# Moving the second row gathers, the activation loads and one norm step in a two-layer mixer and expert kernel

## The chip, the cores and the metric

The kernel runs on one core of a Trainium2 chip. Its engines are TensorE (PE in the profile; its weight loads PEld), VectorE (DVE), ScalarE (ACT), GpSimd (POOL) and SyncE (SP); each runs its own list of instructions in order and meets the others at semaphores. 16 DMA engines move data between the chip's main memory and the on-chip memory; here SyncE issues nearly all plain loads and stores, ScalarE the stores of the gate matrices, and GpSimd the row gathers. The metric is the device time of one execution in microseconds, the median of several.

## What is computed

Two layers over 512 tokens of width 1024, everything in float32. Each layer takes a modulation (shift, scale, gain) from `silu(c) @ ada_w`, runs a token mixer (a chunked state-space scan, a multi-scale pool and stick-breaking attention), and then a product-key expert layer, which is where most of the time goes:

```python
sc = jnp.einsum('thid,hikd->thik', q, keys)          # 8 heads, two halves of 128 keys
top_s, top_i = lax.top_k(sc, 16)
... # top 16 of the 16 x 16 sums, softmax over them: experts (of 16384) and gates
act = jnp.einsum('thkd,td->thk', u_tab[eb], hb)
coef = gb * jax.nn.gelu(act, approximate=False)
out = jnp.einsum('thk,thkd->td', coef, v_tab[eb])
```

So each token uses 128 (8 x 16) of 16384 experts, each with a row of `u_tab` and one of `v_tab`.

## The kernel before

**Tiling.** All tokens stand as columns, and weights come as a stream of tiles of 128 x 1024 (512 KB), 298 a layer: 18 for the input projection, 8 for the output projection, 16 for the queries, 128 for `u` (the U stage, from `U0`) and 128 for `v` (the V stage, from `EV0`). A tile of float32 is split in two parts of float32r: ScalarE writes the high part (`hi`, line 693), VectorE the low part (`lo`, line 1519), and TensorE multiplies three times (high by high, high by low, low by high), 24 matmuls for a tile of the V stage (`v_block`, line 1478).

**Two ways for the experts.** 144 of the 512 tokens (128 and `EXTRA` = 16) go by gathers: GpSimd fetches for each the rows of `u` and of `v` that it needs (`gather`, line 657), 144 gathers of 128 rows of 4 KB (512 KB) for each table and layer, into a ring of five buffers; VectorE multiplies and sums them (`gather_u` line 1998, `gather_v` line 2010). The other 368 tokens (`TD`) go densely through all 16384 experts: the U stage makes their activations, stores them (`activations` in main memory) and builds dense gate matrices (stored too); the V stage reads both back for a group of four tiles (`GROUP`) at a time, multiplies them to coefficients (`coefs`, lines 2101 to 2105), splits these (`c_hi` line 945, `c_lo` line 2111) and multiplies them with the tiles of `v`.

**The V stage on VectorE.** Iteration b does, in this order: the coefficients of tile b+2, one or two gathers (`V_GATHERS[b]`; 144 over 126 iterations, so 18 iterations have two), the low part of the coefficients of b+2, and the low part of weight tile b+2. Before the change the iterations with two are those with b % 7 == 2, that is 2, 9, 16 and so on to 121.

**The order on SyncE.** `load_w(l, n)` has three buffers (`RAWS`): it waits until both parts of tile n-3 are made, so tile b of the V stage is issued at the end of VectorE's iteration b-5. `load_acts(l, g)` (736 KB, line 548) has two buffers and waits until the coefficients of the group two back are made (`s_cp`); `load_gates` (512 KB, line 554) stands right behind it and has no wait of its own there. In the V stage both stand ahead of `load_w` for the tiles 6, 10, 14 and so on. Writing a tile's number as 4m+1, 4m+2 and so on, the group m+1 is loaded, before the change, between the loads of tiles 4m+1 and 4m+2:

```python
if EV0 + 6 <= n < STREAM - 2 and (n - EV0 + 2) % GROUP == 0:
    load_acts(l, (n - EV0 + 2) // GROUP)
    load_gates(l, (n - EV0 + 2) // GROUP)
load_w(l, n)
```

The wait of `load_acts` for group m+1 is for the coefficients of tile 4m-1, which VectorE makes at the start of iteration 4m-3.

**The start.** In layer 0 the first third of the modulation is a product with eight chunks of `adaw` (1 MB each, `ada_chunk`, line 1035, in the order `FIRST_ADA` = 0, 2, 1, 4, 3, 6, 5, 7). `norm_groups` (line 1000) sums the squares of x, ScalarE and VectorE make the inverse root, and `norm_rows` (line 1007) spreads it over the partitions. After the last chunk ScalarE copies the sums (`ada_rows`, line 726), TensorE transposes them (`modulation`, line 1046), and VectorE makes the scales (line 1579) and the normed and modulated columns (lines 1537 and 1545), for which it needs both `modulation` and `norm_rows`; `project_pair` (line 986) multiplies them with the first two weight tiles. VectorE stands at the low part of weight tile 1 before it waits for `modulation`.

Of the kernel before, what the change touches and what calls it, by code (L numbers as in the profile page):

```python
# [34 lines left out]
N_KEYS = 128  # L35
# [3 lines left out]
EV0 = U0 + N_KEYS  # L39
STREAM = EV0 + N_KEYS  # L40
# [14 lines left out]
FIRST_ADA = (0, 2, 1, 4, 3, 6, 5, 7)  # L55
# [13 lines left out]
GROUP = 4  # L69
# [52 lines left out]
    U_GATHERS[_n] = 2 if _n % 3 == 2 else 1  # L122
U_GATHERS[GATHER0] += UG - sum(U_GATHERS)
assert sum(U_GATHERS) == UG and U_GATHERS[N_KEYS - 1] == 0, sum(U_GATHERS)
V_GATHERS = [0] + [2 if _b % 7 == 2 else 1 for _b in range(1, N_KEYS - 1)] + [0]
assert sum(V_GATHERS) == UG


# [55 lines left out]
def build(nc, xT, cT, final_g, adaw, wst, params, keysT, u_0, u_1, v_0, v_1, g_dram, a_dram, outT):  # L184
    u_rows, v_rows = (u_0, u_1), (v_0, v_1)
    ctx = ExitStack()
    with ctx:
# [332 lines left out]
        @block.sync  # L520
        def _(sp):
            sp.dma_start(cond[:, :], cT).then_inc(s_cin, 16)
            for h in range(2):
                half = slice(h * KT // 2, (h + 1) * KT // 2)
                sp.dma_start(x[:, half, :], xT[:, half, :]).then_inc(s_in[h], 16)

            def load_w(l, n):

                g = l * STREAM + n
                if g >= RAWS:  # L530
                    sp.wait_ge(s_wh, g - RAWS + 1)
                    sp.wait_ge(s_wl, g - RAWS + 1)
                sp.dma_start(w_raw[:, g % RAWS, :], wst[l, n]).then_inc(s_raw[g % RAWS], 16)

            def store_act(l, p):

                sp.wait_ge(s_taken, l * TAKEN + p * 2 + (U0 + 4))
                sp.dma_start(a_dram[p], act_out[:, p % 2, :, :]).then_inc(s_ast[p % 2], 16)

            def load_acts(l, g):  # L540

                s = g % 2
                if g >= 2:

                    sp.wait_ge(s_cp, l * N_KEYS + (g - 1) * GROUP)
                for q in range(2):
                    sp.wait_ge(s_ast[q], (l * GROUPS + g + 1) * 16)
                sp.dma_start(act_in[s][:, :, :, :], a_dram[g * 2:g * 2 + 2].rearrange("q p b t -> p q b t")
                             ).then_inc(s_ain[s], 16)

            def load_gates(l, g):

                s = g % 2
                sp.dma_start(gates[s][:, :, :, :],
                             g_dram[:, :, g * GROUP:(g + 1) * GROUP, :].rearrange("c p b t -> p c b t")
                             ).then_inc(s_gin[s], 16)

            sp.dma_start(par[:, :], params[0]).then_inc(s_par, 16)
            for k in (1, 3, 5):
                sp.dma_start(ada_place(k), adaw[0, k]).then_inc(s_ada0[k], 16)  # L560
            load_w(0, 0)
            sp.dma_start(ada_place(7), adaw[0, 7]).then_inc(s_ada0[7], 16)
            load_w(0, 1)
            load_w(0, 2)
            sp.dma_start(fin_g[:, :], final_g).then_inc(s_fgin, 16)

            for l in range(LAYERS):
                for n in range(0 if l > 0 else RAWS, STREAM):
                    if l > 0 and n == RAWS:

                        sp.wait_ge(s_gate, l + 1)
                        sp.dma_start(par[:, :], params[l]).then_inc(s_par, 16)
                    if n == OUT0 + 5:

                        sp.wait_ge(s_ymix, l + 1)
                        sp.dma_start(keys[:, :, :], keysT[l]).then_inc(s_keys, 16)
                    if n == U0 + GATE1 + 8:

                        for s in range(2):
                            sp.wait_ge(s_gst[s], (l + 1) * (GSTORED // 2) * STORES * 16)  # L580
                        sp.wait_ge(s_gv, (l + 1) * QUADS + 2)
                        load_acts(l, 0)
                    if n == U0 + GATE1 + 10:
                        load_gates(l, 0)
                    if n == U0 + GATE1 + 12:
                        load_acts(l, 1)
                    if n == U0 + GATE1 + 14:
                        load_gates(l, 1)
                    if EV0 + 6 <= n < STREAM - 2 and (n - EV0 + 2) % GROUP == 0:
                        load_acts(l, (n - EV0 + 2) // GROUP)  # L590
                        load_gates(l, (n - EV0 + 2) // GROUP)
                    load_w(l, n)
                    if U0 + 6 <= n < EV0 + 6 and n % 2 == 0:
                        store_act(l, (n - U0 - 6) // 2)
            for k in range(KT):
                sp.wait_ge(s_fin, k + 1)
                sp.dma_start(outT[:, k, :], x[:, k, :]).then_inc(s_ret, 16)
            sp.wait_ge(s_ret, KT * 16)
# [357 lines left out]
        def _(pe):  # L956
# [54 lines left out]
            def norm_rows(m):  # L1011

                pe.wait_ge(s_nroot, m + 1)
                root_rows(bank[2], 0).then_inc(s_rows, 1)
# [7 lines left out]
            for l in range(LAYERS):  # L1022
# [31 lines left out]
                if l == 0:  # L1054
                    ada_chunk(0, FIRST_ADA[3])
                if l == 0:
                    for c in FIRST_ADA[4:]:
                        ada_chunk(0, c)
                norm_rows(2 * l)
                if l == 0:  # L1060
                    modulation(0, 0, 4)

                project_pair(l, 0, l * RHS_PARTS)
# [1182 lines left out]
```

## Time and profile before

| | |
|---|---|
| median of 3 runs | 3026.87 us (3025.02 to 3027.24) |
| the profiled execution | 3027.69 us, its span 3025.8 us |
| TensorE busy | 2944.9 us, 97% of the span |
| VectorE, ScalarE, GpSimd busy | 83%, 48%, 32% |
| V stage of layer 0, of layer 1 | from 1019 to 1537 us, from 2491 to 3012 us |
| moved by DMA | 836.79 MB, 277 GB/s over the span |

A row of a timeline gives the start, the duration, the engine, the line, the operation with what it writes and reads, and in brackets the idle time of the engine before it and what ended that. A busy share is that of the engine's records; records of matmuls in a row overlap, since they are pipelined.

### The profile page before, as it was taken

What the parts mean: (1) busy time and instruction counts of PE and PEld (TensorE: products, weight loads), DVE (VectorE), ACT (ScalarE), POOL (GpSimd) and SP (SyncE); (2) the same over time, 40 slices, a digit from 0 to 9 for tenths busy, and PEclk for the clock granted to TensorE, in tenths of its full rate; (3) what the DMA queues carried; (4) which work ended last, traced back from release to release, by engine and by line L of the source; (5) the groups of instructions that cost most, each with busy time, mean ns of one, the idle gap of its engine ahead of it and who ended that gap; (6) DMA issues with size and microseconds to landing.
All of it is one profiled execution on the core that took longest, in us unless ns stands there. A gap on an engine that the chain in (4) does not pass through costs nothing.

```text
span 3025.8 us, 48999 instructions
## 1 busy us (share of the span) xinstructions
PE 2944.9 (97%) x17798; PEld 2760.8 (91%) x17798; DVE 2524.1 (83%) x4842; ACT 1466.4 (48%) x2347; POOL 956.8 (32%) x709
## 2 busy tenths in 40 slices
PE   6999999999999999999989899999999999999998
PEld 4766789999999999999977678999999999999998
DVE  4666789999897789889876669998989868889888
ACT  3353134488884333333343532446888733333333
POOL 0000026544444333233300000565445433333331
PEclk9999999999999999999999999999999999999999
DMA  7424646799999999999931122569999999999996
GB/s 273 176 91 169 255 143 206 249 331 385 350 358 350 352 360 351 365 357 355 359 102 63 56 70 84 165 204 327 353 386 362 311 379 346 358 360 354 355 359 233
DMA packets 252363, 836.79 MB, mean 277 GB/s; under 512 B 24640, under 2 KB 57664, under 8 KB 241472
## 3 DMA queue, kind: packets, MB, share of 16 engines
q1 hardware_dynamic: 158336, 453.50, 42.3%
q0 software_dynamic: 89280, 348.17, 31.1%
q10 hardware_dynamic: 4608, 33.56, 2.6%
q8 instruction: 52, 0.85, 0.1%
q14 instruction: 87, 0.71, 0.1%
HBM read 751.24 MB, written 83.89 MB: 276 GB/s over the span
## 4 chain that ended last, share of the span: by engine, by line
PE 84%; DMA 6%; DVE 6%; ACT 2%; issue 1%; POOL 0%; SPq 0%; DVEq 0%; ACTq 0%; POOLq 0%
PE banks L970 41%; PE banks L1478 28%; PE banks L1446 4%; DMA w_raw<-wst 4%; PE banks L1284 2%; DVE w_lo L1519 2%; PE banks L986 2%; ACT w_hi L693 1%; PE banks L1035 1%; DMA ring<-u,gidx 1%; PE banks L1369 1%; DMA pj<-adaw 1%; PE banks L1255 1%; DVE vacc L2010 1%; PE banks L1460 0%
## 5 line engine op out<-in xcount | busy, mean ns | idle before, releaser
L693 ACT ACTIVATE w_hi<-w_raw 128x1024 fp32r<-128x1024 f32 x596 | 631.6, 1060 | 842.7 <-PE banks L970 638.2
L1519 DVE TENSOR_TENSOR w_lo<-w_raw,w_hi 128x1024 fp32r<-128x1024 f32 x522 | 639.4, 1225 | 360.8 <-ACT w_hi L693 352.0
L970 PE MATMUL banks<-hH,w_hi 128*128 128x368 f32 (+1 forms) x2528 | 881.5, 349 | 7.7 <-ACT w_hi L693 5.1
L970 PE MATMUL banks<-hH,w_lo 128*128 128x368 f32 (+1 forms) x2528 | 861.1, 341 | 0.0
L970 PE MATMUL banks<-hL,w_hi 128*128 128x368 f32 (+1 forms) x2528 | 860.6, 340 | 0.0
L1478 PE MATMUL banks<-c_hi,w_hi 128*128 128x368 f32 x2048 | 676.4, 330 | 5.7 <-DVE w_lo L1519 5.6
L1478 PE MATMUL banks<-c_lo,w_hi 128*128 128x368 f32 x2048 | 674.3, 329 | 0.0
L1478 PE MATMUL banks<-c_hi,w_lo 128*128 128x368 f32 x2048 | 673.2, 329 | 0.0
L657 POOL DMA_INDIRECT ring<-u,gidx x288 | 419.2, 1455 | 453.6 <-DVE gact L1998 419.0
L657 POOL DMA_INDIRECT ring<-v,gidx x288 | 333.7, 1159 | 694.4 <-DVE vacc L2010 631.7
L970 PEld LDWEIGHTS banks<-hH,w_hi 128*128 128x128 f32 x2528 | 475.4, 188 | 52.8 <-issue 20.7
L970 PEld LDWEIGHTS banks<-hH,w_lo 128*128 128x128 f32 x2528 | 474.9, 188 | 19.6
L970 PEld LDWEIGHTS banks<-hL,w_hi 128*128 128x128 f32 x2528 | 475.7, 188 | 17.4 <-issue 0.5
L1478 PEld LDWEIGHTS banks<-c_hi,w_hi 128*128 128x128 f32 x2048 | 384.4, 188 | 8.8 <-issue 8.8
L1478 PEld LDWEIGHTS banks<-c_hi,w_lo 128*128 128x128 f32 x2048 | 384.5, 188 | 0.0
L1478 PEld LDWEIGHTS banks<-c_lo,w_hi 128*128 128x128 f32 x2048 | 384.4, 188 | 0.0
L945 ACT ACTIVATE c_hi<-htok 128x368 fp32r<-128x368 f32 x252 | 129.6, 514 | 518.7 <-DVE htok L2105 513.3
L2010 DVE SCALAR_TENSOR_TENSOR vacc<-ring,gcoef,vacc 128x1024 f32<-128x1024 f32 x284 | 363.7, 1281 | 3.8
L1998 DVE CUSTOM_DVE_ANT_0 ring<-ring,htok 128x1024 f32<-128x1024 f32 x288 | 344.5, 1221 | 19.8 <-DMA ring<-u,gidx 17.3
L645 POOL TENSOR_TENSOR w_lo<-w_raw,w_hi 128x1024 fp32r<-128x1024 f32 x74 | 177.9, 2405 | 520.5 <-ACT w_hi L693 520.5
L889 ACT ACTIVATE oneh<-oneh,idxT 128x128 f32<-128x128 f32 x736 | 226.2, 397 | 5.8 <-DVE oneh L2020 3.2
L2020 DVE TENSOR_TENSOR oneh<-iota,idxT 128x1024 f32<-128x1024 f32 x184 | 219.7, 1222 | 0.0
(315 smaller groups left out, 2954.0 us busy)
## 6 DMA issues: line engine op xcount, KB each, us to landing
w_raw<-wst SPq DMA_DIRECT2D x596, 512.0 KB
activations<-act_out SPq DMA_DIRECT2D x128, 368.0 KB
act_in<-activations SPq DMA_DIRECT2D x64, 736.0 KB
gate_matrices<-stage ACTq DMA_DIRECT2D x32, 1024.0 KB
gates<-gate_matrices SPq DMA_DIRECT2D x64, 512.0 KB
ada_buf<-adaw POOLq DMA_DIRECT2D x24, 1024.0 KB, 6.9
nrm<-adaw POOLq DMA_DIRECT2D x8, 1024.0 KB, 5.3
pj<-adaw POOLq DMA_DIRECT2D x7, 1024.0 KB, 7.1
```

What stands on the lines that cost most here:

```text
L645: pool.tensor_tensor(w_lo[g % 2][:, :, :].rearrange("p a b -> p (a b)"), w_raw[:, g % RAWS, :], w_hi[g % 2][:, :, :].rearrange("p a b -> p ...
L657: pool.indirect_dma_start(out=ring[:, n % RING, :], out_offset=None, in_=rows[:, :], in_offset=bass.IndirectOffsetOnAxis(ap=gidx[:, k % UG ...
L693: nc.scalar.activation(w_hi[g % 2][:, :, :].rearrange("p a b -> p (a b)"), w_raw[:, g % RAWS, :], ACT.Copy).then_inc(s_wh, 1)
L889: ins = nc.scalar.activation(oh, oh, ACT.Copy, scale=idxT[:, 2, q * QUAD + t:q * QUAD + t + 1])
L945: nc.scalar.activation(c_hi[:, (b + 2) % GROUP, :], coef[:, b % 2, :], ACT.Copy).then_inc(s_chi, 1)
L970: last = mm(bank[s][:, 0:t.stop - t.start], a[s][:, k, :], b[:, k, t], start=(k == 0 and a is w_hi and b is hH), stop=(k == KT - 1 and a i ...
L1446: last = mm(bank[2 + u % 2][:, t * P:(t + 1) * P], oneh[u % OH_SLOTS][:, 0, t, :], oneh[u % OH_SLOTS][:, 1, t, :], start=True, stop=True)
L1478: last = mm(bank[k][:, TG:T], w[j % 2][:, k, :], c[:, j, :], start=(first and w is w_hi and c is c_hi), stop=(final and w is w_lo))
L1519: v.tensor_tensor(w_lo[g % 2][:, :, :].rearrange("p a b -> p (a b)"), w_raw[:, g % RAWS, :], w_hi[g % 2][:, :, :].rearrange("p a b -> p (a ...
L1998: v.tensor_tensor_reduce(ring[:, n % RING, :], ring[:, n % RING, :], rhs[:, :], 1.0, 0.0, ALU.mult, ALU.add, gact[:, k:k + 1]).then_inc(s_ ...
L2010: ins = v.scalar_tensor_tensor(acc[:, :], ring[:, n % RING, :], gcoef[:, k:k + 1], acc[:, :], ALU.mult, ALU.add)
L2020: v.tensor_tensor(oneh[q % OH_SLOTS][:, :, :, :], iota[:, :].unsqueeze(1).unsqueeze(1).broadcast_to(full), idxT[:, 0:2, q * QUAD:(q + 1) * ...
```

## The change

Three edits. The iterations with two gathers of the V stage become those with b % 8 == 1, and 61 and 125 besides (again 18). `load_acts` is issued ahead of the load of tile 4m+1 in place of 4m+2; `load_gates` stays where it was. In layer 0 `norm_rows` stands ahead of the last chunk of the first modulation.

```diff
-V_GATHERS = [0] + [2 if _b % 7 == 2 else 1 for _b in range(1, N_KEYS - 1)] + [0]
+V_GATHERS = [0] + [2 if _b % 8 == 1 or _b % 64 == 61 else 1 for _b in range(1, N_KEYS - 1)] + [0]
...
+                    if EV0 + 5 <= n < STREAM - 3 and (n - EV0 + 3) % GROUP == 0:
+                        load_acts(l, (n - EV0 + 3) // GROUP)
                     if EV0 + 6 <= n < STREAM - 2 and (n - EV0 + 2) % GROUP == 0:
-                        load_acts(l, (n - EV0 + 2) // GROUP)
                         load_gates(l, (n - EV0 + 2) // GROUP)
                     load_w(l, n)
...
                 if l == 0:
-                    for c in FIRST_ADA[4:]:
+                    for c in FIRST_ADA[4:7]:
                         ada_chunk(0, c)
                 norm_rows(2 * l)
                 if l == 0:
+                    ada_chunk(0, FIRST_ADA[7])
                     modulation(0, 0, 4)
```

## Rows read from the trace of the kernel before

**Rows 1.** The page: busy time of the engines.

```profile
PE 2944.9 (97%) x17798; PEld 2760.8 (91%) x17798; DVE 2524.1 (83%) x4842; ACT 1466.4 (48%) x2347; POOL 956.8 (32%) x709
```

**Rows 2.** Windows, both V stages: length; busy PE, PEld, DVE, ACT, POOL; clock; DMA share; GB/s.

```profile
1019.00:1531.00 512.00, 510.43 (x3052) 509.28 (x3051) 457.98 (x777) 198.47 (x257) 161.17 (x139) 1.00 0.96 351
2491.00:3006.40 515.40, 511.25 (x3052) 509.29 (x3052) 457.81 (x777) 199.32 (x257) 160.72 (x139) 1.00 0.94 346
```

**Rows 3.** Waits of TensorE in the V stages, layer 0, then 1: total, times, longest.

```profile
PE banks L1478 <- DVE w_lo L1519: 1.5, 2, 0.9
PE banks L1478 <- DVE w_lo L1519: 4.2, 5, 1.3
```

**Rows 4.** Timeline of TensorE at the start of tile 78, layer 0.

```profile
1333.58 0.43 PE L1478 MATMUL banks<-c_hi,w_hi 128*128 128x368 f32 x1 [0.94 <-DVE w_lo L1519]
```

**Rows 5.** Timeline of ScalarE, high parts: tiles 22 and 78 (layer 0), 106 (layer 1).

```profile
1105.09 1.06 ACT L693 ACTIVATE w_hi<-w_raw 128x1024 fp32r<-128x1024 f32 x1 [2.32 <-DMA w_raw<-wst]
...
1330.96 1.06 ACT L693 ACTIVATE w_hi<-w_raw 128x1024 fp32r<-128x1024 f32 x1 [2.75 <-DMA w_raw<-wst]
...
2918.99 1.06 ACT L693 ACTIVATE w_hi<-w_raw 128x1024 fp32r<-128x1024 f32 x1 [2.75 <-DMA w_raw<-wst]
```

**Rows 6.** Timeline of SyncE's queue around the loads of tiles 77 and 78.

```profile
1315.89 0.33 SPq L533 DMA_DIRECT2D w_raw<-wst  x1
1316.43 0.38 SPq L548 DMA_DIRECT2D act_in<-activations  x1
1316.86 0.46 SPq L554 DMA_DIRECT2D gates<-gate_matrices  x1
1319.45 0.34 SPq L533 DMA_DIRECT2D w_raw<-wst  x1
```

**Rows 7.** Groups of instructions, 1030 to 1520 us: gathers taken by VectorE.

```profile
L2010 DVE SCALAR_TENSOR_TENSOR vacc<-ring,gcoef,vacc 128x1024 f32<-128x1024 f32 x139 | 178.0, 1281 | 1.9
```

**Rows 8.** Timeline of VectorE, iteration 72 of layer 0, with two gathers.

```profile
1311.55 2.67 DVE L2010 SCALAR_TENSOR_TENSOR vacc<-ring,gcoef,vacc 128x1024 f32<-128x1024 f32 x2
...
1314.59 1.22 DVE L1519 TENSOR_TENSOR w_lo<-w_raw,w_hi 128x1024 fp32r<-128x1024 f32 x1
```

**Rows 9.** Timeline of ScalarE, high parts: tiles 14, 42 (layer 0), 14 (layer 1).

```profile
1071.19 1.06 ACT L693 ACTIVATE w_hi<-w_raw 128x1024 fp32r<-128x1024 f32 x1 [0.48 <-PE banks L1478]
...
1184.60 1.06 ACT L693 ACTIVATE w_hi<-w_raw 128x1024 fp32r<-128x1024 f32 x1 [0.90 <-DMA w_raw<-wst]
...
2545.20 1.06 ACT L693 ACTIVATE w_hi<-w_raw 128x1024 fp32r<-128x1024 f32 x1 [2.06 <-issue]
```

**Rows 10.** Timelines at the end of layer 0's V stage: VectorE, TensorE.

```profile
1525.66 1.28 DVE L2010 SCALAR_TENSOR_TENSOR vacc<-ring,gcoef,vacc 128x1024 f32<-128x1024 f32 x1
...
1529.12 1.28 DVE L2010 SCALAR_TENSOR_TENSOR vacc<-ring,gcoef,vacc 128x1024 f32<-128x1024 f32 x1
...
1531.03 0.27 PE L1483 MATMUL banks<-ident,vacc 128*128 128x128 f32 x1
```

**Rows 11.** Timelines at the start of the kernel: TensorE, ScalarE, VectorE.

```profile
31.69 1.93 PE L1035 MATMUL banks<-pj,tiny 128*32 128x512 f32 x8 [3.67 <-DMA pj<-adaw]
33.55 2.08 PE L1007 MATMUL banks<-nrm,ident 128*128 128x128 f32 x8
35.42 1.71 PE L1046 MATMUL banks<-ident,ada_row 128*128 128x4 f32 x8
...
33.69 0.60 ACT L726 ACTIVATE ada_row<-banks 128x512 f32<-128x512 f32 x1 [3.48 <-PE banks L1035]
...
35.26 1.23 DVE L1519 TENSOR_TENSOR w_lo<-w_raw,w_hi 128x1024 fp32r<-128x1024 f32 x1 [3.79 <-ACT w_hi L693]
37.16 0.17 DVE L1579 TENSOR_TENSOR mod<-banks,par 128x16 f32<-128x16 f32 x1 [0.68 <-PE banks L1046]
```

**Rows 12.** Windows at the start; the columns are those of rows 2.

```profile
37.20:43.30 6.10, 3.08 (x7) 2.48 (x8) 5.86 (x12) 2.83 (x4) 0.00 (x0) 0.50 0.26 86
43.30:52.00 8.70, 8.70 (x39) 7.18 (x38) 8.53 (x17) 2.91 (x4) 1.09 (x2) 0.99 0.35 119
```

## The prediction

> **What bounds the kernel now.** I read the page first: TensorE is busy for 97% of the span [rows 1], so an edit pays only where TensorE stands still or where its work comes sooner. Then the windows of the two V stages, where two of the three edits lie: 510.43 of 512.00 us busy in layer 0 and 511.25 of 515.40 us in layer 1, at the full granted clock, with the DMA engines 96% and 94% busy [rows 2]. The same 127 tiles take 3.4 us more in layer 1. The waits of TensorE name the cause: in all 7 waits it stood for a low part of weights, 1.5 us in layer 0 and 4.2 us in layer 1 [rows 3]. The recorded idle time is a little too small, since a matmul's record outlasts the start of the next: layer 1 has 4.15 us idle against 1.57, which is 2.6 more, three waits more, and is 3.4 us longer, so each wait moves the end by its idle time and about 0.2 us. **The V stages thus lose 5.7 + 7 x 0.2 = 7.1 us in both layers together. That is all that the two V edits can bring**, 0.23% of the time; the rest is matmuls back to back.
>
> Whose wait is it? At tile 78 TensorE stood 0.94 us for the low part [rows 4]; before that ScalarE had stood 2.75 us, and what ended this was the landing of the weight tile [rows 5]. VectorE only passes it on. ScalarE's long waits of this kind, over 1.7 us, are nine: tiles 22, 50, 78 and 106 of layer 0 (2.32, 1.75, 2.75, 1.91 us) and of layer 1 (2.39, 3.16, 2.78, 2.75), of which three stand in rows 5, and tile 14 of layer 1 (2.06, its releaser not resolved [rows 9]). All are tiles 4m+2, loaded behind activations and gates. SyncE's queue shows it for m = 19: tile 77 at 1315.89, activations 1316.43, gates 1316.86, tile 78 at 1319.45 [rows 6], so 512 + 736 + 512 KB are ahead of tile 78 in one queue. That holds for every m, though; what sets 22, 50, 78 and 106 apart is the second gather, which falls in iterations 16, 44, 72 and 100, that is 4m-4, just before the activations go out in 4m-3.
>
> **A rule for the cost of a late tile.** Tile 78: ScalarE idle 2.75 us, TensorE's start late by 0.94 + 0.2. So the first 1.6 us or so of ScalarE's idle time are covered by its lead over TensorE (an ordinary tile has 0.48 [rows 9]). With 1.65 us as the cover, the eight tiles give 19.8 - 8 x 1.65 = 6.6 us and tile 14 gives 0.4, together 7.0 us, which meets the 7.1 us above. I use this rule for what follows.
>
> **Part 1, the second gathers.** A gather taken costs VectorE 1.28 us (1281 ns [rows 7]) and sends GpSimd to fetch the next 512 KB. The number stays 18, so VectorE's and the DMA's totals stay. No second gather falls in 4m-4 any more: the 6.6 us of the eight tiles go. The new places are b = 1, 9, 17 and so on to 121, and 61 and 125. All of them are of the form 4m-3: the iteration in which the coefficients release SyncE's activation load. For m = 1, 3, ... 29 and for m = 16 there is such a load, 16 a layer, **32 events in all, where the kernel before has 8 of this kind** (m = 3, 10, 17, 24). These 8 are the nearest rows there are. ScalarE's idle time before their tile 4m+2 (14, 42, 70, 98) was 0.48, 0.90, 0.48, 0.93 us in layer 0 and 2.06, 0.92, 0.55, 0.73 in layer 1; three of them stand in the rows [rows 9]. By the rule only the 2.06 costs, 0.4 us. In such an iteration the low part comes 3.0 us after the first gather began (1311.55 to 1314.59 [rows 8]), 1.4 more than with one gather; all 36 second gathers of the kernel before had this delay, and TensorE waited at none for that reason alone, since its waits are at the late tiles. So I cost the delay itself at nothing; its cover is VectorE's slack of 54 us of 512 [rows 2].
>
> **Part 2, the activation loads.** Ahead of tile 4m+1 the load does not go out sooner: its wait for the coefficients of 4m-1 is met only after VectorE's iteration 4m-3 has begun, while tile 4m+1 was free to go at the end of 4m-4. In rows 6 tile 77 went at 1315.89 and the activations, as soon as they could, at 1316.43. With the change SyncE waits 0.54 us with tile 4m+1 queued behind the wait, then issues activations, tile 4m+1 (about 1316.9), gates, tile 4m+2. **Ahead of tile 4m+2 stand the same bytes as before**, and the queue starts on them 0.54 us later. If the DMA engines have gathers to move meanwhile, this costs nothing; if not, tile 4m+2 lands 0.54 us later. I take the 0.54, since around 1314 to 1318 us VectorE had only just released the gathers. Then the eight idle times above become 1.02, 1.44, 1.02, 1.47, 2.60, 1.46, 1.09 and 1.27 us, and by the rule only 2.60 costs, 0.95 us, which is 0.12 us an event: **32 x 0.12 = 3.8 us come back**. The ends: nothing, if the 2.06 was a stray; and, if tile 4m+2 lands a full 1.0 us later, costs of 0, 0.25, 0, 0.3, 1.4, 0.3, 0 and 0.1, 0.3 us an event, 9.4 us in all. That the activations lie ready earlier is worth nothing, as VectorE never waited for them. At the even m without a second gather the 0.54 is covered, as there the idle time lies near 0.5.
>
> **The end of the stage.** Iteration 125 gets a second gather, and TensorE's last tile needs all sums. In layer 0 the last gather was taken from 1529.12 to 1530.4, TensorE asked for the sums at 1531.03 [rows 10]. With two gathers from 1525.66 on, an iteration lasts about 4.2 us to the next gather [rows 8], so the last one ends at about 1531.1: 0.15 us late in each layer, 0.3 us.
>
> **Part 3, the root rows.** TensorE waited 3.67 us for the last chunk, ran it in 1.93 us, then the root rows in 2.08 and the transposes from 35.42, and VectorE went on at 37.16 [rows 11]. The root was ready before that wait, so the rows move into it and vanish. The transposes then wait for ScalarE's copy, which ends at 34.3, and VectorE could go on at 34.35 + 1.74 = 36.1. But it works on the low part of weight tile 1 from 35.26 to 36.49 [rows 11]: this is late next, and the lead is 37.16 - 36.5 = 0.66 us. TensorE's clock was 0.50, the 1.2 GHz level, up to 43.3 us and 0.99 from there [rows 12]; if it comes back at the same time, about half of the lead is lost again (0.3 us stays). If the rows in the pause keep the clock at the 2.4 GHz level for the chunk, this takes about 1.0 in place of 1.93 us, everything behind it moves by 0.9 and the lead is 1.5. Between 0.3 and 1.5 I take 0.6, next to the 0.66 that the rows give. The Trainium skill (TensorE: Matmul & The Clock Gate, Part 1: The HAM clock gate) says that the gate follows how busy the engine has lately been; by it the end with 1.5 us would be possible, and the sum 0.9 us lower.
>
> **Sum:** -6.6 - 0.4 + 3.8 + 0.3 - 0.6 = **-3.5 us**. The profiled execution took 3027.69 us, 0.8 above the median of 3026.87; I take the difference off the median: **3023.4 us**, with 3019 to 3028 as this case's own range by the ends named.
>
> **Rivals.**
> 1. *The stalls simply go.* The 0.54 us is hidden by gathers in flight and the 2.06 us at tile 14 was a stray: -7.0 + 0.3 - 0.6 = -7.3 us, 3019.6. For it: seven of the eight nearest events cost nothing. Against: the DMA engines are 94 to 96% busy, and every second group now meets a second gather. Chance 0.27.
> 2. *The price goes with the gathers.* The DMA engines are at 96%; each of the 36 second gathers costs its part (7.0 / 36 = 0.19 us) wherever it stands, since it is one more transfer against the weights: -7.0 + 32 x 0.19 + 0.3 - 0.6 = -1.2 us, 3025.7. Chance 0.18.
> 3. *The tile behind the activations becomes the late one*, and the kernel gets slower. Tile 4m+1 goes out 1.0 us later and behind 736 KB. From 1315.89 until tile 78 was there at 1330.96, 15.1 us, its queue moved 2.33 MB; activations and tile 4m+1 are 1.28 MB, 8.3 us by that rate, from 1316.43 to 1324.7. Tile 77 was due 4.0 us before tile 78, whose due time was 1330.96 - 2.3 = 1328.7, so at 1324.7: no slack is left. If two tiles are late in each of the 32 events and TensorE loses 0.5 us, the sum is -7.0 + 16 + 0.3 - 0.6 = +8.7 us, 3035.6. It decides from a mean loss of 0.23 us an event, that is 1.9 us of mean idle time of ScalarE before the tile. Against: the 15.1 us were of the worst kind of group, and the new kind begins its burst before its gathers. Chance 0.10. The Trainium skill (DMA: Bandwidth & Descriptors, Queues, rings and completion order) has each DMA engine start the descriptors of a ring in order and take turns between rings; it speaks for this rival, because tile 4m+1 cannot pass the activations, and it would give the 3035.6.
>
> **How the numbers follow.** My forecast has 0.45. Less than 0.2% (6.05 us) is about what a measurement of this kernel can't tell from no change, so faster means under 3020.8: rival 1 and a small part of the forecast, 0.30. Slower means over 3032.9: rival 3, 0.10. The rest, 0.60, is within. The range from 3018.8 to 3029.0 takes in rivals 1 and 2 and the ends of the forecast; it leaves out rival 3 and a start that gives more than 1.5 us.
>
> **What would show it.** After the change TensorE's waits for low parts at tiles 22, 50, 78 and 106 are gone; ScalarE's longest waits for weight tiles stand at 4m+2 with odd m and are mostly under 1.6 us; SyncE issues activations at the time it did, tile 4m+1 about 1 us later. Long waits at 4m+1 would show rival 3. At the start VectorE's first scale comes at 36.5. I am wrong if TensorE's waits in the V stages add up to under 1 or over 8 us, or if time moves outside the V stages and the first 55 us.

## The result, and the profile after

| | before | after |
|---|---|---|
| median | 3027.71 us (3025.02 to 3033.58) | 3048.86 us (3037.51 to 3054.06) |
| the profiled execution, its span | 3027.69, 3025.8 us | 3048.42, 3046.5 us |
| V stages, first to last matmul with coefficients, layer 0 and 1 | 518.0 and 521.4 us | 531.1 and 531.9 us |
| TensorE's waits in the V stages | 1.5 + 4.2 us in 7 | 10.2 + 11.0 us in 20 |

The changed kernel is **slower: ratio 1.0061, 95% interval 1.0044 to 1.0079**. 3023.4 us was forecast, in a range up to 3029.0; the result lies outside it. Of the 20.7 us by which the span grew, the V stages have +23.6; the rest of the kernel is 2.9 us shorter, which is no finding, since between the two V stages the traces below differ by up to 6.6 us (951.3 to 957.9 us) with nothing changed there.

Waits of TensorE in the two V stages after (total, times, longest), which answer to rows 3:

```profile
PE banks L1480 <- DVE w_lo L1521: 10.2, 10, 2.9
PE banks L1480 <- DVE w_lo L1521: 11.0, 10, 2.5
```

The windows of rows 2 at their new places, with the same columns:

```profile
1017.90:1529.90 512.00, 501.76 (x2975) 497.79 (x2974) 445.10 (x760) 192.51 (x250) 159.34 (x139) 1.00 0.94 346
2501.20:3016.60 515.40, 504.27 (x2990) 500.33 (x2989) 447.48 (x763) 194.21 (x252) 158.94 (x139) 1.00 0.94 345
```

In the same 512 us TensorE ran 2975 matmuls where it had run 3052 [rows 2]: 77 less, 3.2 tiles, 13 us. The engine waited for is the same as before, VectorE's low part, and the one behind it too. Timeline of ScalarE, the high parts of tiles 22 and 78 (layer 0) and 38 (layer 1), answering to rows 5:

```profile
1105.78 1.06 ACT L694 ACTIVATE w_hi<-w_raw 128x1024 fp32r<-128x1024 f32 x1 [3.83 <-DMA w_raw<-wst]
...
1340.53 1.06 ACT L694 ACTIVATE w_hi<-w_raw 128x1024 fp32r<-128x1024 f32 x1 [2.34 <-DMA w_raw<-wst]
...
2658.90 1.06 ACT L694 ACTIVATE w_hi<-w_raw 128x1024 fp32r<-128x1024 f32 x1 [3.90 <-DMA w_raw<-wst]
```

All are tiles 4m+2 of groups with a second gather in iteration 4m-3, the 32 events of the prediction. ScalarE's idle time before them was 1.95 us on average (the mean of 32 rows like these), over 1.65 us in 20 of them, and up to 3.90. Before tile 4m+1 it was 0.33 us: the tile behind the activations was not late. SyncE's queue for tiles 21 and 22 of layer 0, answering to rows 6:

```profile
1089.41 0.38 SPq L548 DMA_DIRECT2D act_in<-activations  x1
1089.88 0.54 SPq L533 DMA_DIRECT2D w_raw<-wst  x1
1090.46 0.61 SPq L554 DMA_DIRECT2D gates<-gate_matrices  x1
1093.62 0.33 SPq L533 DMA_DIRECT2D w_raw<-wst  x1
```

Activations, tile 21, gates and tile 22, as described in the prediction: 1.05 us from the first to the third issue where rows 6 have 0.97.

### The profile page after: what moved, and what is told of

Read it like the earlier page. It is cut to its first block, busy times and chain, and to the rows that moved or that the text cites. A ratio compares the mean times of both kernels' runs of the same rounds, so it can differ in the third digit from the quotient of the medians.

```text
span 3046.5 us, 48999 instructions
## 1 busy us (share of the span) xinstructions
PE 2952.5 (97%) x17798; PEld 2763.2 (91%) x17798; DVE 2522.8 (83%) x4842; ACT 1462.6 (48%) x2347; POOL 953.5 (31%) x709
## 4 chain that ended last, share of the span: by engine, by line
PE 73%; DMA 12%; DVE 8%; ACT 3%; issue 3%; POOL 0%; SPq 0%; DVEq 0%; ACTq 0%; POOLq 0%
PE banks L971 40%; PE banks L1480 18%; DMA w_raw<-wst 10%; PE banks L1448 4%; DVE w_lo L1521 3%; PE banks L1286 2%; ACT w_hi L694 2%; PE banks L987 2%; DVE vacc L2012 2%; PE banks L1036 1%; DMA ring<-u,gidx 1%; PE banks L1371 1%; DMA pj<-adaw 1%; PE banks L1257 1%; PE banks L1462 0%
## 5 line engine op out<-in xcount | busy, mean ns | idle before, releaser
L1480 PE MATMUL banks<-c_hi,w_hi 128*128 128x368 f32 x2048 | 679.8, 332 | 21.4 <-DVE w_lo L1521 21.2
```

Of the source, the lines that this page charges most:

```text
L1480: last = mm(bank[k][:, TG:T], w[j % 2][:, k, :], c[:, j, :], start=(first and w is w_hi and c is c_hi), stop=(final and w is w_lo))
```

## The experiments

Beside the ratio, the table at the end of this section gives for each kernel the length of both V stages together in its trace. That is the finer number: TensorE's own pace leaves 1030.5 us for them (the least of all these traces), and what is above is waiting and, behind some waits, a lower clock. It comes from one execution of each kernel, though: two traces of the changed kernel differ by 8.4 us in it (1063.0 and 1054.6), so a small difference in it counts only where the ratios agree.

### Which of the three edits

**e1_gathers_only**

```diff
-V_GATHERS = [0] + [2 if _b % 7 == 2 else 1 for _b in range(1, N_KEYS - 1)] + [0]
+V_GATHERS = [0] + [2 if _b % 8 == 1 or _b % 64 == 61 else 1 for _b in range(1, N_KEYS - 1)] + [0]
```

> The second gathers stand at b % 8 == 1, 61 and 125 as in the changed kernel; the activation loads and the root rows stay as before. The changed kernel was 0.6% (about 20 us) above the kernel before. Theory A (the places of the second gathers cost: in each group with a second gather in 4m-3 the DMA falls behind): 12 to 25 us above before, TensorE's waits for low parts in the V stages 20 us or more. Theory B (only the activations ahead of tile 4m+1 cost): by the rule of the prediction 1 to 7 us below before, waits under 5 us. Theory C (both are needed together): within 3 us of before.

Measured: ratio 0.9996 (0.9986 to 1.0005), 3024.0 us; V stages 1033.6 us, 5.8 less than before. Waits of TensorE, both V stages:

```profile
PE banks L1478 <- DVE w_lo L1519: 0.5, 1, 0.5
PE banks L1478 <- DVE w_lo L1519: 0.4, 2, 0.2
```

Timeline of SyncE's queue for tiles 21 and 22, and ScalarE's high part of tile 22:

```profile
1091.91 0.33 SPq L533 DMA_DIRECT2D w_raw<-wst  x1
1092.45 0.38 SPq L548 DMA_DIRECT2D act_in<-activations  x1
1092.88 0.54 SPq L554 DMA_DIRECT2D gates<-gate_matrices  x1
1096.67 0.35 SPq L533 DMA_DIRECT2D w_raw<-wst  x1
...
1105.96 1.06 ACT L693 ACTIVATE w_hi<-w_raw 128x1024 fp32r<-128x1024 f32 x1 [0.96 <-DMA w_raw<-wst]
```

Tile 22 was split 9.3 us after its issue here, and 12.2 us after it in the changed kernel (1093.62 to 1105.78), with the same bytes ahead of it and GpSimd's gathers at the same distance. Over the 32 events the idle time before tile 4m+2 is 0.98 us, over 1.65 in four. So the stalls of part 1 of the prediction go. The whole time shows less of it than the trace: by the ratio it is 1.2 us below before, with an interval from 4.2 below to 1.5 above.

**e2_acts_only**

```diff
+                    if EV0 + 5 <= n < STREAM - 3 and (n - EV0 + 3) % GROUP == 0:
+                        load_acts(l, (n - EV0 + 3) // GROUP)
                     if EV0 + 6 <= n < STREAM - 2 and (n - EV0 + 2) % GROUP == 0:
-                        load_acts(l, (n - EV0 + 2) // GROUP)
```

> The activation loads go out ahead of tile 4m+1; second gathers (b % 7 == 2) and root rows as before. Theory A: within 3 us of before. Theory B: 12 to 25 us above. Theory C: 0 to 8 us above, since only four groups a layer have a second gather in 4m-3. In every case the activations should be issued at the time they were, and tile 4m+1 about 1 us later.

Measured: 1.0046 (1.0031 to 1.006), 3039.97 us; TensorE waited 2.6 us in 5 and 7.9 us in 10. Most of the loss comes with this edit alone, as theory B of the two expectations has it; theory A and theory C (0 to 8 us) are out. With the old gathers mainly two kinds of group carry it: those with the second gather in 4m-3 (mean idle time before tile 4m+2 1.49 us, where it was 0.88) and those with it in 4m-4, where now tile 4m+1 is the late one (2.01 us) and no longer 4m+2 (0.66). That is the mechanism of rival 3, but only in 8 groups, and not in the changed kernel, which has no second gather there.

**e3_norm_only**: in layer 0 `norm_rows` ahead of the last chunk, nothing else (the third part of the diff).

> Only the root rows of the first norm stand ahead of the last chunk. VectorE's first scale comes 0.7 us sooner if the clock of the chunk stays low, 1.5 us if it stays at the upper level; the first pair of tiles then ends 0.3 to 1.5 us sooner. The whole time within the spread of the runs of before.

Measured: 3028.84 us, which alone tells nothing at this size; the trace does. The start of the changed kernel, which has the same order, TensorE, ScalarE and VectorE, answering to rows 11:

```profile
27.81 1.16 PE L1008 MATMUL banks<-nrm,ident 128*128 128x128 f32 x8
31.76 1.06 PE L1036 MATMUL banks<-pj,tiny 128*32 128x512 f32 x8 [2.79 <-DMA pj<-adaw]
32.89 0.60 ACT L727 ACTIVATE ada_row<-banks 128x512 f32<-128x512 f32 x1 [2.63 <-PE banks L1036]
34.47 1.23 DVE L1521 TENSOR_TENSOR w_lo<-w_raw,w_hi 128x1024 fp32r<-128x1024 f32 x1 [2.95 <-ACT w_hi L694]
35.61 0.17 DVE L1581 TENSOR_TENSOR mod<-banks,par 128x16 f32<-128x16 f32 x1
```

A window of the pause ahead of the last chunk, columns as in rows 2, first of the kernel before, then of the changed one:

```profile
28.00:31.60 3.60, 0.02 (x3) 0.00 (x0) 1.23 (x1) 1.06 (x1) 0.00 (x0) 0.75 1.00 407
```

```profile
28.00:31.60 3.60, 0.97 (x8) 0.78 (x7) 1.23 (x1) 1.06 (x1) 0.00 (x0) 1.00 1.00 407
```

The root rows run in the pause, the granted clock stays at 1.00, the 2.4 GHz level, where before it fell (0.75 over the stretch), the last chunk takes 1.06 us in place of 1.93, ScalarE's copy and with it the low part of weight tile 1 move up too, and VectorE's first scale comes at 35.61, 1.55 us earlier (1.64 in e3).

**e10_both_loops**: e1 and e2 together, without the root rows.

> The changed kernel with the root rows where they were: both edits of the V stage. If the root rows have no part in the loss: 18 to 24 us above before, as the changed kernel (or 1 to 2 us more than that one). If it is within 10 us of before, the root rows' edit takes part.

Measured: 1.0065 (1.0052 to 1.0078), V stages 1063.2 us. This is the changed kernel (1.0061, 1063.0): the root rows have no part in the loss. The two V edits together cost 0.23% more than the sum of their parts (-0.04% and +0.46%), which with these intervals is only just clear of noise.

### What in the load edit costs

Ahead of tile 4m+1 now stand a wait (0.54 us, for the coefficients of tile 4m-1) and 736 KB. The next kernels part them.

**e9_gathers_and_wait**: the gathers of e1, the loads in the old order, and the wait alone moved up:

```diff
+                    if EV0 + 5 <= n < STREAM - 3 and (n - EV0 + 3) % GROUP == 0:
+                        sp.wait_ge(s_cp, l * N_KEYS + ((n - EV0 + 3) // GROUP - 1) * GROUP)
```

> Second gathers at b % 8 == 1, 61, 125 and SyncE waiting for the coefficients ahead of tile 4m+1, loads in the old order (tile 4m+1, activations, gates, 4m+2), root rows as before. It lies between the kernel with the gathers alone (0.9996) and the changed one (1.0061). With the gathers alone ScalarE's idle time before tile 4m+2 in the 32 groups with a second gather was 0.98 us in the mean, in the changed kernel 1.95. Theory D (the wait makes all of it): mean 1.8 or more, 15 us or more above before. Theory O (the order makes all of it): mean under 1.2, within 3 us. If each makes about half: mean 1.4 to 1.6 and 4 to 10 us above before.

Measured: 1.0043 (1.003 to 1.0056), V stages 1055.5 us. Waits of TensorE, both stages:

```profile
PE banks L1480 <- DVE w_lo L1521: 9.9, 9, 2.9
PE banks L1480 <- DVE w_lo L1521: 7.5, 9, 2.0
```

The mean idle time before tile 4m+2 is 1.82 us. From e1 to the changed kernel it grows by 0.97 us; 0.84 of that is here with no load moved. Whether the order adds the rest isn't shown: the ratios (1.0043 here, 1.0065 in e10) have intervals that touch, and the second trace of the changed kernel (e16, below) has 1.65 us and V stages of 1054.6, less than this one.

**e5_wait_only**: the same wait, in the kernel before with its old gathers.

> Kernel before, but SyncE waits for the coefficients ahead of tile 4m+1, and then issues in the old order: tile 4m+1, activations later, ahead of 4m+2. It keeps the delay of tile 4m+1 (about 0.5 us) and drops the new order. Theory D (the delay of the whole burst makes the tiles late): at least two thirds of the cost of the activation edit, 9 us or more above before. Theory O (the order costs: tile 4m+1 stands behind 736 KB): within 4 us of before.

Measured: 1.0023 (1.0011 to 1.0035). Its trace (3.5 us of waits in 4, 1.2 in 2) is that of its fastest execution, 9 us under its median, and shows too little. The 7 us lie between the two expectations: under the 9 of theory D, over the 4 of theory O. With 8 groups of the kind 4m-3 the wait costs 0.23%, with 32 of them 0.47% (e1 to e9).

**e13_wait_for_tile_before**: e9, with the wait for one tile earlier, so that it never holds anything.

```diff
-                        sp.wait_ge(s_cp, l * N_KEYS + ((n - EV0 + 3) // GROUP - 1) * GROUP)
+                        sp.wait_ge(s_cp, l * N_KEYS + ((n - EV0 + 3) // GROUP - 1) * GROUP - 1)
```

> The new gathers and SyncE's extra wait ahead of tile 4m+1, but for the coefficients of tile 4m-2 in place of 4m-1. These are made an iteration earlier, so the instruction stands in the queue and never holds tile 4m+1. If it is the 0.54 us of delay that costs, this is the kernel with new gathers alone: ratio 0.998 to 1.001, ScalarE's idle time before tile 4m+2 about 1.0 us on average, TensorE's waits in the V stages under 2 us. If the wait instruction itself (or the way that it spaces the issues) costs, it is like the kernel with the wait of 0.54 us: ratio 1.003 to 1.006 and about 17 us of waits.

Measured: 1.0001 (0.999 to 1.0013), V stages 1033.2 us, mean idle time 1.06 us, TensorE's waits 1.2 us. As expected for a cost of the hold: the instruction costs nothing, holding tile 4m+1 back by 0.54 us does.

**e14_wait_for_first_gather**: e9, with the wait until VectorE has taken the first gather of iteration 4m-3.

```diff
-                        sp.wait_ge(s_cp, l * N_KEYS + ((n - EV0 + 3) // GROUP - 1) * GROUP)
+                        sp.wait_ge(s_gd, l * GATHERS + UG + sum(V_GATHERS[:n - EV0 - 4]) + 1)
```

> The new gathers and SyncE's extra wait ahead of tile 4m+1, now until VectorE has taken the first gather of iteration 4m-3: 0.54 + 1.3 = about 1.9 us after tile 4m+1 was free to go, in place of 0.54. If each microsecond of delay moves tile 4m+2 by one microsecond, ScalarE's mean idle time before it is 0.98 + 1.9 = 2.9 us, which by the cover of 1.65 us costs about 1.2 us an event and 40 us in 32: ratio 1.012 to 1.015. If the delay counts 1.6 to 1.8 times, as between the kernels without and with the wait of 0.54 us (0.84 to 0.97 us later), it is 4 us and 75 us: ratio 1.02 or more. If what costs is mainly that the burst is issued in one piece just ahead of the two gathers, whatever the delay, the mean stays near 2 to 2.5 us and the ratio near 1.005 to 1.008.

Measured: 1.0043 (1.0027 to 1.006). Waits of TensorE, both stages:

```profile
PE banks L1480 <- DVE w_lo L1521: 2.8, 6, 0.6
PE banks L1480 <- DVE w_lo L1521: 2.5, 6, 0.5
```

The mean idle time before tile 4m+2 is 1.01 us and the V stages take 1042.0 us. None of the three expectations came about: the least of them had 2 us. Timelines of SyncE's queue and of GpSimd around tile 21, and TensorE's start of tile 27:

```profile
1091.48 0.33 SPq L533 DMA_DIRECT2D w_raw<-wst  x1
1091.91 0.40 SPq L548 DMA_DIRECT2D act_in<-activations  x1
1092.36 0.48 SPq L554 DMA_DIRECT2D gates<-gate_matrices  x1
...
1091.72 1.94 POOL L659 DMA_INDIRECT ring<-v,gidx  x1 [3.29 <-DVE vacc L2012]
1093.96 1.28 POOL L659 DMA_INDIRECT ring<-v,gidx  x1 [0.30 <-issue]
...
1127.51 0.43 PE L1480 MATMUL banks<-c_hi,w_hi 128*128 128x368 f32 x1 [0.52 <-DVE w_lo L1521]
```

**e15_first_gather_again**: the same kernel, for a second trace.

> The kernel of e14 once more, for a second trace. If lateness goes by where the burst stands against the gathers, ScalarE's idle time before tile 4m+2 is again near 1.0 us on average (0.8 to 1.3) and TensorE's waits in the V stages are 4 to 9 us. If it goes by the delay and e14's trace was a lucky one, the mean is 1.8 us or more and the waits are over 15 us.

Measured: 3030.86 us, mean idle time 1.10 us, 6 of 32 over 1.65, waits 3.4 us in 7 and 3.0 in 7, V stages 1043.0 us.

**e16_changed_again**: the changed kernel, for a second trace.

> The changed kernel once more, for a second trace. If its lateness is settled by where the burst stands, the mean idle time before tile 4m+2 is again 1.8 to 2.1 us with 17 to 25 of 32 over 1.65 us, though the tiles concerned may be others. If it is chance, it is elsewhere between 1.0 and 2.5 us.

Measured: 3046.75 us, mean idle time 1.65 us, 15 of 32 over 1.65, waits 7.9 us in 10 and 6.8 in 8, V stages 1054.6 us. The mean and the count are under what was expected, so a trace has some 0.3 us of its own in this number. The changed kernel (1.95, 1.65) and that of e14 (1.01, 1.10) stay apart.

I set the issue of tile 4m+1 against the moment when GpSimd issues the first gather of iteration 4m-3 (means of 32 events; tile 4m+2 goes out 2.69 us after that moment in every one of these kernels):

| kernel | tile 4m+1 issued, against that moment | idle before 4m+2 | V stages |
|---|---|---|---|
| e1, e13 | 1.99 us before | 0.98, 1.06 us | 1033.6, 1033.2 |
| e9 | 1.45 before | 1.82 | 1055.5 |
| changed, its second trace | 0.97 before | 1.95, 1.65 | 1063.0, 1054.6 |
| e14, e15 | 0.29 before | 1.01, 1.10 | 1042.0, 1043.0 |

**The lateness of tile 4m+2 does not grow with the delay.** A hold of 0.54 us makes it 0.84 us later, one of 1.7 us hardly at all. What counts is how the burst of loads and the two gathers meet. The issue of the gates, the last load ahead of tile 4m+2, tells the same against the same moment: 1.01 us before it in e1, 0.53 in e9, 0.39 in the changed kernel, 0.62 us behind it in e14. The eight such events of the kernels with the old gathers fit in: 1.20 us before it with 0.88 us of idle time in the kernel before, 0.69 with 1.37 in e5, 0.64 with 1.49 in e2. That is an order of rows and no mechanism yet.

**The whole time of e14 is no better than that of e9**, 1.0043 both. Its waits are of two kinds: eight of the twelve, 3.7 of 5.3 us, are at tiles 4m+3, as the tile 27 shown, before which ScalarE was not idle; there VectorE itself was late. And its ratio says 13 us where its stages say 3 more than before; the rest of it I can't place.

### Where the second gathers stand

**e4_gathers_phase3**: the kernel before with the second gathers in iterations b % 8 == 3, and 63 and 119, that is 4m-1, two iterations behind the burst.

> Second gathers at b % 8 == 3, 63 and 119, that is in iterations 4m-1, two iterations after the activation loads are released; loads and root rows as before. Theory A, and the reading that a second gather hurts by what it takes from the DMA engines just before tile 4m+2: 3 to 7 us below before, nearly no waits of TensorE in the V stages. If a second gather costs the same wherever it stands (rival 2 of the prediction): within 2 us of before, 5 to 8 us of waits.

Measured: 0.9977 (0.9967 to 0.9987), no wait of TensorE for a low part in either V stage, V stages 1030.7 us; ScalarE's idle time before tile 4m+2 is 0.05 us in those groups.

**e12_gathers_phase0**: the same with b % 8 == 0, and 4, 60 and 124, that is 4m-4, just ahead of the burst.

> Second gathers at b % 8 == 0, 4, 60 and 124, that is in iterations 4m-4, where the kernel before had eight and lost 0.83 us at each; loads and root rows as before. If the place makes the loss, about 33 events at 0.8 us lose 26 us, less the 7 us of before: 15 to 25 us above before, with the waits at tiles 4m+2. If rival 2 of the prediction holds (a second gather costs the same everywhere): within 3 us of before.

Measured: 1.0062 (1.0047 to 1.0076). TensorE's waits, both V stages:

```profile
PE banks L1478 <- DVE w_lo L1519: 9.4, 12, 1.4
PE banks L1478 <- DVE w_lo L1519: 4.0, 7, 1.4
```

Timeline of ScalarE, the high parts of tiles 22 and 38, two out of a pattern of every eighth tile:

```profile
1103.37 1.06 ACT L693 ACTIVATE w_hi<-w_raw 128x1024 fp32r<-128x1024 f32 x1 [2.16 <-DMA w_raw<-wst]
...
1169.38 1.06 ACT L693 ACTIVATE w_hi<-w_raw 128x1024 fp32r<-128x1024 f32 x1 [2.72 <-DMA w_raw<-wst]
```

As many second gathers as before and as in e4, and 1.0062 against 0.9977: rival 2, a price that goes with a gather wherever it stands, is false. The reading of rows 5 and 6, that the place 4m-4 makes the long stalls, is right: 26 of the 32 groups that have both a second gather there and a load of activations have over 1.65 us.

**e7_acts_phase3**: the gathers of e4 with the activations moved as in the change.

> Activations ahead of tile 4m+1 as in the changed kernel, second gathers in iterations 4m-1 (b % 8 == 3, 63, 119), root rows as before. If the two edits work together (a second gather within the activation burst is what the early loads can't bear), it is within 3 us of before. If the early loads cost by themselves, it is 8 to 16 us above the kernel with the second gathers in 4m-1 alone, which was at a ratio of 0.9977.

Measured: 0.9989 (0.9979 to 0.9999). Against e4 the edit costs 0.12% here, which is not clear of noise; against e1 it cost 0.65%. With no second gather at the burst there is little for the earlier wait to collide with.

### What stands ahead of the tile

**e6_split_gates**: the kernel before, with the gates one tile later, behind tile 4m+2.

```diff
                     if EV0 + 6 <= n < STREAM - 2 and (n - EV0 + 2) % GROUP == 0:
                         load_acts(l, (n - EV0 + 2) // GROUP)
-                        load_gates(l, (n - EV0 + 2) // GROUP)
+                    if EV0 + 7 <= n < STREAM - 1 and (n - EV0 + 1) % GROUP == 0:
+                        load_gates(l, (n - EV0 + 1) // GROUP)
```

> Kernel before, but the gate loads go out one tile later, ahead of 4m+3, so that only 736 KB stand ahead of tile 4m+2 in place of 1248 KB. If the bytes in the queue ahead of tile 4m+2 make it late, TensorE's 7 us of waits in the V stages fall to under 3 us and the time is 3 to 6 us below before. If the DMA engines as a whole are the limit, the waits move to 4m+3 and the time stays within 2 us.

Measured: 0.9972 (0.9961 to 0.9984), no wait for a low part, V stages 1030.6 us, with the old second gathers in 4m-4 and all. That is somewhat more than the 3 to 6 us expected, and the waits did not move to 4m+3.

**e11_changed_gates_later**: the changed kernel with the same move.

> The changed kernel with the gate loads one tile later, ahead of 4m+3. Ahead of tile 4m+2 then stand activations and tile 4m+1, 512 KB less. If what makes 4m+2 late is how much is queued ahead of it, ScalarE's idle time before it falls from 1.95 to under 1.0 us in the mean, TensorE's waits from 21 to under 6 us, and the time is within 5 us of before. If the late start of the burst is all that matters, it stays at 15 us or more above.

Measured: 0.9977 (0.9967 to 0.9987), V stages 1031.4 us. The only wait for a low part in the two V stages:

```profile
PE banks L1480 <- DVE w_lo L1521: 0.3, 1, 0.3
```

Timeline of ScalarE, the high part of tile 22:

```profile
1106.95 1.06 ACT L694 ACTIVATE w_hi<-w_raw 128x1024 fp32r<-128x1024 f32 x1 [0.48 <-PE banks L1480]
```

The early wait, the activations ahead of 4m+1 and the gathers in 4m-3 are all still there; 512 KB behind the tile in place of ahead of it take 0.84% off (1.0061 to 0.9977), and no tile 4m+2 is over 1.65 us. The tile that now stands behind the gates, 4m+3, has 0.62 us.

**e8_split_phase3_norm**: gates later, second gathers as in e4, root rows as in the change.

> Gate loads one tile later, second gathers in 4m-1, root rows ahead of the last chunk. TensorE's waits in the V stages were already nearly gone with the second gathers in 4m-1 alone (ratio 0.9977); the split can add little there, the root rows about 1 us: 6 to 9 us below before. If the gates now come too late for the coefficients, VectorE would show waits for gates and the time would rise.

Measured: 0.9971 (0.9956 to 0.9985), V stages 1030.5 us. Not measurably better than e6 or e4 alone: each of the two heals all that there is, and the root rows are too small to be seen. e6, two lines, is the version to keep.

| kernel | ratio | V stages, both |
|---|---|---|
| before | 1 | 1039.4 us |
| changed | 1.0061 | 1063.0 |
| e1 gathers only | 0.9996 | 1033.6 |
| e2 activations only | 1.0046 | 1047.1 |
| e9 gathers and wait | 1.0043 | 1055.5 |
| e12 gathers ahead of the burst | 1.0062 | 1051.8 |
| e4 gathers behind the burst | 0.9977 | 1030.7 |
| e6 gates behind the tile | 0.9972 | 1030.6 |
| e11 changed, gates behind the tile | 0.9977 | 1031.4 |

## Why the prediction was wrong

**What bounds the kernel: right.** 7.1 us were named as all that the V edits can bring. e4, e6 and e8, without one such wait, bring the stages from 1039.4 to 1030.5 us, 8.9 us, and the whole time 7 to 9 us down (0.9977 to 0.9971).

**The rule for a late tile: right in kind, low in size.** A cover of 1.65 us of ScalarE's idle time gives 21.3 us for the changed kernel, and the rule meant the whole loss, the 0.2 us beside each wait included. TensorE's recorded waits are 21.2 (1.5 of them at three tiles 4m+3, where VectorE itself was late, which the rule doesn't know). With about 0.2 us for each of the 20 they are 25.2, and with 3.3 us for the clock (below) 28.5, where the stages are 32.5 over the floor of 1030.5 us; 4 us stay unplaced. Before it is 7.1 and 8.9.

**Part 1: right for the stalls.** The eight nearest rows have 0.4 us by the rule, 1.6 us for 32 events in 4m-3, and e1 shows 0.7 us for all 32. Its V stages are 5.8 us shorter than before, its whole time by a ratio of 0.9996 only 1.2. The stalls of the old second gathers are gone where none stands any more (50, 106). 22 and 78, which I counted among the cured, belong to odd m and have a second gather in 4m-3 now.

**Part 2: this is the step that failed.** It said that tile 4m+2 lands 0.54 us later and that this costs 0.12 us an event, at most 0.3. Measured is 0.97 us later (0.98 to 1.95; 0.67 in the second trace) and, by the prediction's own rule, 0.67 us an event, 21.3 us for 32 in place of 3.8. With this one term put right the prediction's sum is +14.0 us in place of -3.5; the ratio of 1.0061 is +18.5 us, and the rest is no more than what the rule itself falls short by. From e1 to the changed kernel the V stages grow by 29.4 us. The fault has two parts. First the shift: I moved a wait, saw 0.54 us of hold, and took the landing to move by at most that or, for the upper end, 1.0 us. e9 and e13 show that the hold is the cause, e14 and e15 that it doesn't act as a delay: with 1.7 us the tile is as early as with none. So no row of the kernel before could price it by adding times. Then the price: for the end with 1.0 us I had eight rows, of which seven lay between 0.48 and 0.93 us, and I moved them up together. In the changed kernel the idle times scatter from 0.47 to 3.90 us, and with a cover of 1.65 only the upper tail costs: a tail that eight rows with one outlier (2.06, which one end of the range set aside as a stray) can't show. The 32 idle times of e1 moved up together by 0.54 us cost 5.3 us by the rule, by 0.97 us 12.2; the rest up to 21.3 is scatter. The outlier was the warning: it showed that an event of this kind can go over the cover by itself.

**The sentence "ahead of tile 4m+2 stand the same bytes as before"** is true, and was read the wrong way. It says that moving the activations can't help that tile; it doesn't say that the tile is safe. The same bytes were its trouble, as e6 and e11 show.

**Part 3: right in size.** The lead at VectorE is 1.55 us, the upper end: the clock stayed at the 2.4 GHz level in the pause. The Trainium skill (TensorE: Matmul & The Clock Gate, Part 1: The HAM clock gate) has the gate follow how busy TensorE has lately been; the trace agrees in this pause, with 1.00 where it was 0.75. But the first pair of weight tiles ran at the 1.2 GHz level from 38.65 to about 43.6 us, where before it did so from 40.22 to 43.4 [rows 12]: 1.8 us more at half pace, which gives 0.9 back. 0.65 us remain by this sum (0.6 was taken), and the traces show it: from 46 us on TensorE's matmuls start 0.71 us earlier in the changed kernel, 0.52 in e3. That is less than any whole time here can show.

**The end of the stage: right.** 0.15 us a layer was forecast; the stretch from TensorE's last matmul with coefficients ahead of the first sums to the next one behind them grew from 0.42 to 0.59 us.

**The rivals.** Rival 1 is what e1 does to the stalls with the gathers alone (0.9 us of waits are left of 5.7), though its whole time does not show the 7.3 us. Rival 2 is false (e4, e12). Rival 3 had the sign, a tenth of the chance and 8.7 us of the 18.5; it named the right edit and asked for 1.9 us of mean idle time to decide, which is what came about (1.95). But it put this at tile 4m+1 or both, and tile 4m+1 was never late here (at most 1.25 us of idle time before it, 0.33 on average): the changed kernel split it 8.5 us after its issue on average, and that of e14 7.7 us after it. The Trainium skill's rule that it leaned on (DMA: Bandwidth & Descriptors, Queues, rings and completion order), that descriptors of a ring start in order, does not by itself tell which tile of a burst suffers.

**What stays open** is why the meeting of burst and gathers makes tile 4m+2 late. Over 14 us, from 2 us before GpSimd issues the first gather of iteration 4m-3, the DMA engines moved 4.82 MB on average in the changed kernel, 4.80 in e9, 4.88 and 4.90 in e1 and e13. But it was 4.76 in e14, where the tile was early, and 4.88 in the second trace of the changed kernel, where it was late; so it is not simply a smaller throughput. At tile 22 alone it looks as if it were. Windows of the changed kernel, six microseconds from the issue of the activations and the next six (the last two numbers are DMA share and GB/s), and the same of e13:

```profile
1089.40:1095.40 6.00, 6.00 (x38) 6.00 (x37) 5.90 (x9) 2.80 (x4) 3.21 (x2) 1.00 0.82 257
1095.40:1101.40 6.00, 6.00 (x38) 6.00 (x37) 5.62 (x12) 1.80 (x3) 1.99 (x2) 1.00 1.00 359
```

```profile
1090.20:1096.20 6.00, 6.00 (x38) 6.00 (x37) 5.89 (x9) 2.79 (x4) 3.22 (x2) 1.00 0.91 322
1096.20:1102.20 6.00, 6.00 (x38) 6.00 (x37) 5.62 (x12) 1.82 (x3) 1.99 (x2) 1.00 1.03 402
```

The kernel takes a tile as landed when its semaphore has grown by 16 (`then_inc(..., 16)` in `load_w`); how far the last of these steps lies behind the first the trace doesn't tell. The Trainium skill (DMA: Bandwidth & Descriptors, Two DMAs through the same engine are not ordered) says that nothing orders transfers across the 16 engines, which leaves room for this; no run here shows it.

## What to carry to other kernels

Here a burst in one DMA queue made late what stood at its end, and the cure was to take bytes from ahead of that tile (e6, e11) or other traffic from around the burst (e4), not to issue parts of it sooner. A wait that is moved up a queue moves everything behind it against the traffic of other queues, and here its length was no measure of what that cost: treat a moved wait ahead of a nearly saturated burst as unpriced, and ask for the number of events times the distance to the cover, not for the mean. When one of a few nearest rows is already over the threshold, price all the new events by that row for one end of the range: 2.60 us, which costs 0.95, times 32 is 30 us here, and such a range would have held what came.

## What the runs showed of the hardware beyond that

**The clock can fall inside a stage that is nearly always busy.** After the stall at tile 22 TensorE, which had worked back to back for tens of microseconds, came back at half pace. Timeline of TensorE in the changed kernel:

```profile
1106.05 0.33 PE L1480 MATMUL banks<-c_hi,w_lo 128*128 128x368 f32 x1
1108.40 0.51 PE L1480 MATMUL banks<-c_hi,w_hi 128*128 128x368 f32 x1 [2.02 <-DVE w_lo L1521]
1108.70 0.51 PE L1480 MATMUL banks<-c_lo,w_hi 128*128 128x368 f32 x1
...
1111.46 0.51 PE L1480 MATMUL banks<-c_lo,w_hi 128*128 128x368 f32 x1
1111.77 0.45 PE L1480 MATMUL banks<-c_hi,w_lo 128*128 128x368 f32 x1
1112.05 0.33 PE L1480 MATMUL banks<-c_hi,w_hi 128*128 128x368 f32 x1
```

Windows of the changed kernel behind three stalls, tiles 22 and 62 of layer 0 and 38 of layer 1; the third number from the end is the granted clock:

```profile
1108.60:1112.00 3.40, 3.40 (x12) 3.40 (x12) 3.40 (x8) 1.46 (x2) 1.00 (x1) 0.50 0.62 210
1277.50:1281.00 3.50, 3.50 (x21) 3.50 (x22) 3.40 (x7) 1.46 (x2) 1.71 (x1) 1.00 0.59 169
2661.70:2665.00 3.30, 3.30 (x12) 3.30 (x12) 3.30 (x7) 1.46 (x2) 0.99 (x1) 0.50 0.58 183
```

Twelve matmuls at a pitch of 0.31 us in place of 0.17: 1.6 us lost on top of a stall of 2.0 us, and 1.7 in layer 1 behind the stall at tile 38. Three other stalls of about this size or longer (2.93 us at tile 62 and, in layer 1, 1.90 and 2.06 at 14 and 22) left the clock at 1.00, so such a stall makes the fall possible and not certain. Over all traces of this case the clock fell six times in the V stages ahead of the last sums, each time behind a stall of 2.0 to 2.6 us, and stayed up behind five others of 2.0 to 2.9 us. The Trainium skill (TensorE: Matmul & The Clock Gate, HAM oscillation — how this bites in real kernels) describes waits for DMA after which the next work starts at the low clock; the trace agrees, with TensorE's wait for a low part that a late load holds up, for two stalls of five, at 1.6 and 1.7 us each.

**One and the same load can take 9.3 or 12.2 us** from its issue to its first use, with the same bytes ahead of it, by what the gathers beside it do (tile 22 in e1 and in the changed kernel).
